# A decoder layer with PEER retrieval: first-stage weight chunks multiplied two side by side, projection columns awaited by group, cache copies two a tile, first sample keys loaded a stage earlier

## The reference, cut to what matters

```python
mod = silu(c) @ w_ada + b_ada                 # 9 conditioning rows x 6144
shift1, scale1, gate1, shift2, scale2, gate2 = split(mod, 6)
h = rmsnorm(x, norm1_g) * (1 + scale1) + shift1
aq, ak, av, mqk, mv, mo, mi, mf = split(h @ w_in, SPLITS)      # 3592 columns
att = combine(dilated attention of aq, ak, av)   # samples: over a cache of 2048 keys as well
k_new, v_new = last 2048 rows of (cache, new)    # the caches, moved on by 8 rows
hA = mlstm(short_conv(mqk), mv, gates mi, mf)
x = x + gate1 * (concat(hA, att) @ w_out)
h2 = rmsnorm(x, norm2_g) * (1 + scale2) + shift2
x = x + gate2 * peer(h2)     # 8 heads x 16 experts a token, picked out of 16384, rows gathered
```

## Time and profile before

| | us |
|---|---|
| median of 3 runs | 4123.54 (4121.14 to 4129.88) |
| profiled execution | 4114.69 |
| its span, first to last instruction | 4112.9 |
| TensorE busy | 3490.1 (85%) |
| VectorE busy | 2392.8 (58%) |
| ScalarE busy | 1615.3 (39%) |
| GpSimd busy | 1279.3 (31%) |

### The profile page before, as it was taken

The page is one execution under the profiler, slowest core; times in us unless marked ns, Lnnn a source line. Parts: engine busy times, 40 slices in busy tenths (PEclk is TensorE's granted clock), DMA queues, the critical chain, the costliest instruction groups (busy, mean ns, idle before and its releaser), DMA issues.

```text
span 4112.9 us, 38258 instructions
## 1 busy us (share of the span) xinstructions
PE 3490.1 (85%) x12228; PEld 1766.6 (43%) x12228; DVE 2392.8 (58%) x5587; ACT 1615.3 (39%) x4381; POOL 1279.3 (31%) x1204
## 2 busy tenths in 40 slices
PE   7796999778689789888978988897889789889877
PEld 1353665545335334434534443453445345325321
DVE  1253555326558756955865694487459547847744
ACT  0132233133453463354345335534543453433333
POOL 0000000011334433433443443344344334435433
PEclk9897999789899999999999999999999999999999
DMA  9698011975899999999999999999999999999998
GB/s 374 223 344 283 22 44 36 188 251 193 324 397 402 417 408 396 402 414 395 397 416 393 383 404 391 388 404 414 383 387 400 414 363 396 408 355 415 413 407 367
DMA packets 241246, 1420.21 MB, mean 345 GB/s; under 512 B 42964, under 2 KB 65876, under 8 KB 93316
## 3 DMA queue, kind: packets, MB, share of 16 engines
q0 software_dynamic: 168768, 1200.70, 72.8%
q1 hardware_dynamic: 69972, 198.90, 14.8%
q10 hardware_dynamic: 2304, 18.16, 1.1%
HBM read 1385.48 MB, written 98.73 MB: 361 GB/s over the span
## 4 chain that ended last, share of the span: by engine, by line
PE 27%; DMA 23%; DVE 19%; ACT 8%; issue 2%; POOL 1%; SPq 0%; ACTq 0%; POOLq 0%; DVEq 0%
DMA mem<-in_experts,mem 21%; PE psum L1334 18%; DVE mem L1630 9%; DVE mem L1496 3%; PE psum L1233 3%; DVE mem L1495 3%; PE psum L1251 2%; ACT L1440 1%; ACT mem L1444 1%; DVE mem L1498 1%; ACT mem L1441 1%; PE psum L1208 1%; DMA mem<-qkv_rows 1%; PE psum L1189 1%; ACT mem L1440 1%
## 5 line engine op out<-in xcount | busy, mean ns | idle before, releaser
L1334 PE MATMUL psum<-mem 128*128 128x512 f32 (+1 forms) x4352 | 2138.8, 623 | 420.7 <-ACT mem L1444 419.4
L1630 DVE CUSTOM_DVE_ANT_0 mem<-mem 128x1024 f32<-128x1024 f32 x1088 | 1324.8, 1221 | 794.9 <-DMA mem<-in_experts,mem 782.8
L1159 POOL DMA_INDIRECT mem<-in_experts,mem x1088 | 1213.5, 1115 | 1830.0 <-PE psum L1334 1769.7
L1334 PEld LDWEIGHTS psum<-mem 128*128 128x128 f32 (+1 forms) x4352 | 769.7, 192 | 1470.6 <-ACT mem L1444 770.5
L1440 ACT ACTIVATE mem<-mem 128x1 f32<-128x1 f32 x1088 | 219.5, 202 | 1537.2 <-DVE mem L1630 1534.9
L1444 ACT ACTIVATE mem<-mem 128x128 f32<-128x128 f32 (+1 forms) x1088 | 434.3, 399 | 35.8
L589 PE MATMUL psum<-mem 128*128 128x512 f32 (+3 forms) x864 | 340.7, 546 | 11.0 <-ACT mem L554 9.8
L1441 ACT ACTIVATE mem<-mem 128x1 f32<-128x1 f32 x1088 | 320.4, 294 | 35.3
L1251 PEld LDWEIGHTS psum<-mem 128*128 128x128 f32 x2304 | 276.5, 191 | 61.3 <-issue 57.3
L1251 PE MATMUL psum<-mem 128*128 128x128 f32 (+1 forms) x2304 | 282.1, 275 | 3.3 <-ACT mem L1390 3.0
L589 PEld LDWEIGHTS psum<-mem 128*128 128x128 f32 (+1 forms) x864 | 149.0, 191 | 176.3 <-issue 162.5
(11 more groups left out here) (259 smaller groups left out, 2493.8 us busy)
## 6 DMA issues: line engine op xcount, KB each, us to landing
out_k_s<-in_cache_k SPq DMA_DIRECT2D x8, 4080.0 KB
out_v_s<-in_cache_v SPq DMA_DIRECT2D x8, 4080.0 KB
mem<-in_w_ada SPq DMA_DIRECT2D x12, 2048.0 KB
mem<-mod_rows SPq DMA_DIRECT2D x34, 512.0 KB
mem<-in_experts,mem POOLq DMA_INDIRECT x1088, 9.7
mem<-in_keys_t POOLq DMA_DIRECT2D x16, 1024.0 KB, 6.3
mem<-in_vals POOLq DMA_DIRECT2D x16, 1024.0 KB, 7.8
mem<-in_w_in ACTq DMA_DIRECT2D x8, 1796.0 KB, 40.4
```

The lines of the kernel that those rows point to most:

```text
L1159: pool.indirect_dma_start(out=ring[:, g % N_SLOTS].rearrange("p a n -> p (a n)"), out_offset=None, in_=ins["experts"][:, :], in_offset=bas ...
L1334: mm = nc.tensor.matmul(psum[0:r, half], diag[:, g % 4, 0:r], ring[:, g % N_SLOTS, 1, half * 512:(half + 1) * 512], start=c == 0, stop=c = ...
L1630: v.tensor_tensor_reduce(row, row, h2[i % 2], 1.0, 0.0, ALU.mult, ALU.add, dots[:, c:c + 1]).then_inc(sig["dots"], 1)
```

## The change

Stage 0: `cond` is padded with zeros to 64 columns, and the chunks go in six pairs; of a pair, one chunk's product goes to output partitions 0 to 63 and the other's to 64 to 127, the two alternating step by step. A pair is one of two buffers, and the second buffer lies where the first three eighths of `w_in` go. SP issues a pair when the product before last is done. Bias and gains come in four loads on ACT's queue, ahead of the one-hot rows and tables (three of them from SP's queue). The prompt's bias table is made after the fourth pair. `w_in` comes in three groups of columns: mv, mo and gates; mqk; attention. Its last five eighths of the first two groups are loaded after the fourth pair's product, all else after the last; TensorE waits for each group where tile 0 first uses it. Stage 1: two cache copies on each of tiles 1 to 8; SP loads the first two pieces of sample keys ahead of `w_out`, and ACT loads the samples' rows at its end. Stage 3: these loads are gone from SP and POOL; the index is made in two halves of 64 picks, the first six slots earlier, and POOL waits for each half.

```diff
@@ -195,6 +195,23 @@
 N_ADA = 6 * D // ADA_CHUNK
 
 END_KEPT = W_B + N_KEPT
+
+HALF_PE = 64
+W_IN_PARTS = {"mvo": slice(O_MV, W_IN), "mqk": slice(O_QK, O_MV), "qkv": slice(0, O_QK)}
+
+
+def sample_first(mem):
+
+    at = Region(mem, END_SMALL + 3 * KD * D, MEM)
+    keys, vals = at.take(2, 4, 512), at.take(2, 4, W_B)
+    return keys, vals, vals[0:NS, 0].rearrange("p t n -> p (t n)")[:, 0:2 * W_B]
+
+
+def sample_keys(ins, m):
+
+    b, p = divmod(m, 3)
+    w = min(512, ROWS - 512 * p)
+    return w, ins["keys_t"][b, :, 2048 * p:2048 * p + 4 * w].rearrange("p (j r) -> p j r", j=4)
 
 
 def last_weights(mem):
@@ -240,108 +257,123 @@
 def stage0(nc, block, sig, mem, psum, const, table, ins, scratch):
 
     work = Region(mem, END_W, MEM)
-    cond = work.take(KD, NC9)
-    w = work.take(2, KD, ADA_CHUNK)
-    bias = work.take(2, ADA_CHUNK)
+    cond = work.take(KD, HALF_PE)
+    w_own = work.take(2, KD, ADA_CHUNK)
     gain = work.take(2, ADA_CHUNK)
...
-    rows = work.take(6 * D)
+    rows = work.take(N_ADA // 2, ADA_CHUNK)
     tab = work.take(LTAB)
     w_in = mem[:, END_SMALL:END_W].rearrange("p (k n) -> p k n", k=KD)
+    w_lent = Region(mem, END_SMALL, END_SMALL + 3 * W_IN).take(2, KD, ADA_CHUNK)
...
+    w = (w_own, w_lent)
+    mod_at = (slice(0, NC9), slice(HALF_PE, HALF_PE + NC9))
+    gain_of = {1: 0, 4: 1}
 
     @block.sync
     def _(sp):
         sp.dma_start(cond, ins["cond"]).then_inc(sig["cond_in"], 16)
-        sp.dma_start(table, ins["const"]).then_inc(sig["const_in"], 16)
-        sp.dma_start(onehot, ins["onehot"]).then_inc(sig["onehot_in"], 16)
-        sp.dma_start(rel, ins["rel"]).then_inc(sig["onehot_in"], 16)
...
+        for c in range(N_ADA // 2):
+            if c >= 2:
+                sp.wait_ge(sig["mod_ps"], c - 1)
+            for t in range(2):
+                sp.dma_start(w[c % 2][:, t], ins["w_ada"][2 * c + t]).then_inc(sig[f"ada_in{c % 2}"], 16)
...
     @block.scalar
     def _(act):
+        for t in range(2):
+            b = ins["b_ada"].rearrange("o (c t n) -> o c t n", t=2, n=ADA_CHUNK)[:, :, t]
+            act.dma_start(rows[mod_at[t]], b.broadcast_to((NC9, N_ADA // 2, ADA_CHUNK))).then_inc(sig["mod_small_in"], 16)
+            g = ins["norm_gain"].rearrange("g (t n) -> t g n", t=2)[t:t + 1]
+            act.dma_start(gain[mod_at[t]], g.broadcast_to((NC9, 2, ADA_CHUNK))).then_inc(sig["mod_small_in"], 16)
+        act.wait_ge(sig["cond_in"], 16)
+        nc.scalar.activation(cond, cond, ACT.Silu).then_inc(sig["cond"], 1)
+        act.dma_start(s_rel, ins["s_rel"]).then_inc(sig["s_onehot_in"], 16)
+        act.dma_start(s_hot, ins["s_onehot"]).then_inc(sig["s_onehot_in"], 16)
+        act.dma_start(onehot, ins["onehot"]).then_inc(sig["onehot_in"], 16)
+        act.dma_start(rel, ins["rel"]).then_inc(sig["onehot_in"], 16)
+        act.dma_start(table, ins["const"]).then_inc(sig["small_in"], 16)
...
+
+        def w_in_part(name, k, cols):
+            act.dma_start(w_in[:, k, cols], ins["w_in"][:, k, cols]).then_inc(sig[f"w_in_{name}"], 16)
+
+        act.wait_ge(sig["mod_ps"], 4)
+        for name in ("mvo", "mqk"):
+            w_in_part(name, slice(3, KD), W_IN_PARTS[name])
+        act.wait_ge(sig["mod_ps"], N_ADA // 2)
+        for name in ("mvo", "mqk"):
+            w_in_part(name, slice(0, 3), W_IN_PARTS[name])
+        for k in (slice(0, 4), slice(4, KD)):
+            w_in_part("qkv", k, W_IN_PARTS["qkv"])
+        act.wait_ge(sig["small_in"], 96)
 
     @block.tensor
     def _(pe):
-        pe.wait_ge(sig["onehot_in"], 32)
-        for n, (a, m) in enumerate(pieces):
-            if n >= 2:
-                pe.wait_ge(sig["bias_tab"], n - 1)
-            nc.tensor.matmul(psum[0:H_B, 4 + n % 2, 0:m], rel, onehot[:, a:a + m], start=True, stop=True).then_inc(sig["bias_ps"], 1)
         pe.wait_ge(sig["cond"], 1)
...
+        for c in range(N_ADA // 2):
+            pe.wait_ge(sig[f"ada_in{c % 2}"], 32 * (c // 2 + 1))
+            if c >= 2:
+                pe.wait_ge(sig["mod_row"], 2 * (c - 1))
             for k in range(KD):
-                mm = nc.tensor.matmul(psum[0:NC9, n % 2, :], cond[:, k, :], w[:, n % 2, k, :], start=k == 0, stop=k == KD - 1)
+                for t in range(2):
+                    mm = nc.tensor.matmul(psum[HALF_PE * t:HALF_PE * (t + 1), c % 2, :], cond[:, k, :], w[c % 2][:, t, k, :], start=k == 0, stop=k == KD - 1)
             mm.then_inc(sig["mod_ps"], 1)
-            if n == 3:
+            if c == 1:
...
+            if c == 3:
+                pe.wait_ge(sig["onehot_in"], 32)
+                for n, (a, m) in enumerate(pieces):
+                    if n >= 2:
+                        pe.wait_ge(sig["bias_tab"], n - 1)
+                    nc.tensor.matmul(psum[0:H_B, 4 + n % 2, 0:m], rel, onehot[:, a:a + m], start=True, stop=True).then_inc(sig["bias_ps"], 1)
 
...
+            dve.wait_ge(sig["mod_ps"], c + 1)
+            for t in range(2):
+                out = rows[mod_at[t], c]
+                op = nc.vector.tensor_tensor(out, psum[mod_at[t], c % 2, :], out, ALU.add)
...

 def stage1(nc, block, sig, mem, psum, const, ins, outs, scratch):
@@ -349,7 +381,11 @@
     def weights_in(sp):
 
         w_out, w_q = last_weights(mem)
+        s_keys, _, _ = sample_first(mem)
         sp.wait_ge(sig["av_ps"], NT + 1)
+        for m in range(2):
+            w, src = sample_keys(ins, m)
+            sp.dma_start(s_keys[:, m, :, 0:w], src).then_inc(sig[f"s_first_in{m}"], 16)
         sp.dma_start(w_out, ins["w_out"]).then_inc(sig["w_out_in"], 16)
         sp.dma_start(w_q, ins["w_q"]).then_inc(sig["w_q_in"], 16)
 
@@ -427,10 +463,9 @@
         def tile(i, rows, first):
             sp.wait_ge(sig["h"], i)
             sp.dma_start(x[0:rows], first).then_inc(sig["x_in"], 16)
-            if 1 <= i <= 4:
-                for b in (2 * i - 2, 2 * i - 1):
-                    for name in ("k_s", "v_s"):
-                        sp.dma_start(outs[name][b, 0:WBUF - DS], ins["cache_" + name[0]][b, DS:WBUF]).then_inc(sig["cache_out"], 16)
+            if i >= 1:
+                for name in ("k_s", "v_s"):
+                    sp.dma_start(outs[name][i - 1, 0:WBUF - DS], ins["cache_" + name[0]][i - 1, DS:WBUF]).then_inc(sig["cache_out"], 16)
 
...
@@ -579,6 +614,11 @@
         for i in range(NT):
             tile(i, P, "p")
         tile(NT, NS, "s")
+        _, _, s_raw = sample_first(mem)
+        act.wait_ge(sig["h"], NT + 1)
+        act.wait_ge(sig["av_ps"], NT + 1)
+        act.wait_ge(sig["qkv_out"], 48 * (NT + 1))
+        act.dma_start(s_raw, scratch["qkv"].ap()[SEQ:NTOK, 0:2 * W_B]).then_inc(sig["s_raw_in"], 16)
 
     @block.tensor
     def _(pe):
@@ -601,7 +641,7 @@
         def tile(i, rows, kind):
             pe.wait_ge(sig["h_t"], 2 * i + 2)
             if i == 0:
-                pe.wait_ge(sig["w_in_in"], 16 * KD)
+                pe.wait_ge(sig["w_in_mvo"], 32)
             else:
                 pe.wait_ge(sig["mnew"], i)
             project(i, 7, O_G, 2 * H_A, rows).then_inc(sig["gates_ps"], 1)
@@ -611,6 +651,8 @@
             if i >= 1:
                 pe.wait_ge(sig["hraw"], i)
                 pe.wait_ge(sig["kws"], i)
+            else:
+                pe.wait_ge(sig["w_in_mqk"], 32)
...
@@ -625,6 +667,8 @@
                 turn(i + 1, P if i + 1 < NT else NS)
             if i >= 1:
                 pe.wait_ge(sig["state"], i)
+            else:
+                pe.wait_ge(sig["w_in_qkv"], 32)
             project(i, 2, 0, W_B, rows)
 
             pe.wait_ge(sig["diag_a"], i + 1)
@@ -989,7 +1032,6 @@
-        sp.dma_start(s_raw, scratch["qkv"].ap()[SEQ:NTOK, 0:2 * W_B]).then_inc(sig["s_raw_in"], 16)
         sp.dma_start(s_bias, scratch["s_bias"].ap()).then_inc(sig["s_bias_in"], 16)
 
...
         def s_keys_in(m):
             if m >= 3 * DB:
                 return
...
+            pool.wait_ge(sig["s_s_ps"], m - 1)
+            w, src = sample_keys(ins, m)
             pool.dma_start(s_keys[:, m % 2, :, 0:w], src).then_inc(sig[f"s_keys_in{m % 2}"], 16)
 
         def s_vals_in(m):
@@ -1133,8 +1172,6 @@
                 pool.dma_start(to, s_att[b % 2][64 * a:64 * a + 32]).then_inc(sig[f"s_out{b % 2}"], 16)
 
         nc.gpsimd.memset(s_qbd, 0.0).then_inc(sig["s_qbd_fill"], 1)
-        s_keys_in(0)
-        s_keys_in(1)
         for b in range(DB):
             s_keys_in(3 * b + 2)
             s_keys_in(3 * b + 3)
@@ -1149,11 +1186,13 @@
         pool.wait_ge(sig["s_out0"], 32 * DB // 2)
 
         for i, _ in windows[1:]:
-            pool.wait_ge(sig["idx"], i + 1)
+            pool.wait_ge(sig["idx"], 2 * i + 1)
             if i == NT:
                 pool.wait_ge(sig["pair_idx"], 16)
             for c in range(picks_of(i)):
                 g = i * PICKS + c
+                if c == HALF:
+                    pool.wait_ge(sig["idx"], 2 * i + 2)
                 if g >= N_SLOTS:
                     pool.wait_ge(sig["summed"], g - N_SLOTS + 1)
...
@@ -1265,7 +1304,10 @@
             if m == 0:
```

(17 more changed lines are left out.)

73 lines of the change are left out of this document (22 added, 51 removed).

## The result

The changed kernel took 4049.16 us in the median of four runs (4042.64 to 4053.40), against 4122.34 for the kernel before in four runs beside it: 73.2 us less, a ratio of 0.9823 with a 95% interval of 0.9801 to 0.9846. The forecast was 4043.6, inside 4012 to 4070. The profiled execution took 4053.40, its span 4051.6, at a mean granted clock of 0.95. Five more runs of it in a later comparison gave 4054.71 (0.9841, 0.9818 to 0.9864).

The account below looks back on a forecast made before the run. From about 1,130 us the gathers' DMA, around 400 GB/s, sets the pace, so gains come before it: 32.5 + 42.6 + 4.5 + 0.3 = 79.9 us off the 4123.54 median gives 4043.6 us, range 4012 to 4070.

Parts of the forecast that it names:

- Stage 0 products: Stage 0, TensorE: two chunks side by side on output halves; a pair takes 6.9 us warm, 8.5 after a long wait.
- Rival 1: Stage 0: pairs run at half clock, 1.2 GHz, 13.8 us each; total 57.2 us less, 4066; chance 0.08.
- Stage 0 loads: Stage 0: chunks loaded in pairs, projection weights beside them; rows out at 104.7 instead of 142.75 us, 38.0 us less.
- The end nearest to a row is that where the weights take half or more, as they did: Stage 0, last chunk pair: projection weights take half the DMA or more, all there at 94.8 us; chunks first, 82.1.
- rival 3: Stage 0: DMA serves chunks first, pair 5 at 82.1 us, small transfers pass between the weights; total 4025; chance 0.12.
- The hand-over: Stage 0 to stage 1: rows out under load +1.7 us, 1.57 MB in +3.8; 5.5 us lost, 32.5 left.
- The 1.57 MB in at half rate: Start of stage 1: loads before ScalarE's first x, beside projection weights, come at half rate, 3.8 us more.
- Cache copies: Stage 1: two copies a tile end VectorE's wait on stores; the 104.32 us tile becomes 61.74, 42.6 us less.
- Sample keys and rows: Loads moved from stage 3 into stage 1: 4.5 us won in stage 3, nothing or at most 2 us lost.
- the state's store comes after all of them and ends the stage: nothing, at most 2 us: End of stage 1: the last sample stores have 5 us more beside them; cost nothing, at most 2 us.
- Index in halves: Stage 3: POOL's first gather, which waits 0.89 us for the index, comes 0.3 us sooner.
- its own signs of being wrong: Wrong if a tile exceeds 62 us, pairs take 13.8 us, or the first gather is not about 80 us sooner.

## Why the prediction was right, and where it was not

**Stage 0 products.** As forecast: 7.11 us warm (6.9), 8.8 to 9.9 after waits (8.5); the earlier trace rows were the right place to look, and the halves do run side by side. Rival 1, the lower clock for whole batches, did not come: the second, fourth and sixth pair ran their first 3.4 to 5.6 us at 0.50 and the rest at 1.00, so only part of each was slower, as the forecast held. The Trainium skill (TensorE: Matmul & The Clock Gate, HAM oscillation — how this bites in real kernels) says that a batch after such a wait starts cold again. The trace agrees for the two long waits (6.75 and 3.97 us, clock at 0.50 when the pair starts at 34.48 and 84.53); after the wait of 2.23 us the clock fell some 0.3 us into the pair. That the whole batch would then stay cold was the prediction's reading, not the page's.

**Stage 0 loads.** Forecast 38.0 us, measured 48.0. The step that failed is "The end nearest to a row is that where the weights take half or more, as they did". The row was a load of whole weight rows; the change cuts the columns into groups, and packets of 4.1 KB got 28% of the bytes beside packets of 13.9 KB. That the packets' size made the share is supported by the wider load (34%), not proven. Pair 5 landed at 84.53, not 94.8; rival 3's 82.1, given a chance of 0.12, was nearer, and with no weights beside it at all the pair did land at 82.10.

**The hand-over.** Forecast +5.5 us, measured +11.3: out and barrier 10.8 us instead of 7.75 (+1.7 forecast), in 14.8 instead of 6.6 (+3.8). The step that failed is "The 1.57 MB in at half rate": in 14.8 us they came at about a quarter of 0.417 MB a us. From 95 to 120 us ACT's queue moved 8.21 of 10.07 MB. With 6.3 MB of that taken away the hand-over took 17.3 to 18.4 us in two kernels. The two errors, +10.0 and -5.8, cancel in part, and with the 0.9 us of the first gates' and values' projection leave 35.8 us at the first q/k projection, against 32.5. That these were this close is luck.

**Cache copies.** 42.6 forecast, 42.6 measured between the same two points. By the two experiments the copies alone give all of it on the old stage 0, and 34.5 on the new one, where the stall was 8.1 us smaller already; the prediction took the parts as independent, and the sum does not suffer since the stall goes whole either way.

**Sample keys and rows.** Forecast 4.5 us won in stage 3 and at most 2 lost in stage 1; measured 2.4 won and 4.75 lost, a loss of 2.3. The step that failed is "the state's store comes after all of them and ends the stage: nothing, at most 2 us": the loads come at full rate only 11 us after they are asked for, and then reach into that store. The slow start stood in the trace of the kernel before, from 762 to 774 us, and the sum left it out.

**Index in halves.** The first gather's wait for it, 0.89 us, became 0.30 of plain issue: 0.6, not 0.3. It lies inside the 2.4 us above, and no run takes it alone.

**The sum.** First gather 76.0 us sooner (69.5 in the second trace) against 79.9; medians 73.2 and 67.8. The sample part missed by 6.8 us (2.3 lost for 4.5 won), and stage 0 with its hand-over gave 3.3 of it back. So the total is near by errors of both signs: 10.0 us one way, 5.8, 0.9 and 6.8 the other. By its own signs of being wrong the forecast passes in the first trace; in the second one tile took 63.44 us, over its 62, and the first gather came only 69.5 us sooner, not about 80.

## What to carry to other kernels

Where two queues load at once, ask how large the packets of each are before sharing out the bandwidth: here a load of 4.1 KB packets got 28% beside one of 13.9 KB, and the small stores and broadcasts of the hand-over got 1.86 of 10.07 MB. A load that is moved "into cover" must be followed to the end of the cover. Three such moves here met the next transfer that someone waits for: the weights beside the hand-over (11.3 us longer), the sample's keys ahead of the state's store (2.3 us lost in all), and the attention columns beside the copies (a wait of 26 us). The transfers that nobody waits for are the first to hold back or spread: the copies' new pace is the largest part that an experiment shows by itself (42.6 us on the old stage 0, 34.5 on the new).

## What the runs showed of the hardware that was not expected

In seven of the thirteen traces one tile of stage 1, not always the same, took 63.4 us instead of 61.74, and in two more the first took 65.1, with no new wait of TensorE in it. In all nine it was the same group of products that grew, the projection of the gates and values at the end of the tile: 10.52 us (12.18 in the two) instead of 8.82. In the second trace of the changed kernel it was the stretch from 566 to 577 us, at a granted clock of 0.84:

```profile
566.00:577.00 11.00, 11.00 (x40) 6.05 (x40) 4.04 (x11) 6.77 (x17) 1.81 (x4) 0.84 0.38 145
```

Inside it the clock was 0.50 from 569 to 572 us and 1.00 again from 573. Just before the clock fell, TensorE did short products of 129 columns with waits of 1.1 to 1.2 us between them, then the gates' products of 8 columns. Every tile has the same products and waits, the same place in the tile before had 1.00, and most tiles never dip; why one does isn't known.
